# Low halves of the weights: subtracted on GpSimd in place of VectorE

## The reference

```python
for layer in range(2):
    mod = silu(c) @ ada_w[layer] + ada_b[layer]            # 2048 x 6144
    shift, scale, gate = split(mod, 3)
    h = rms_norm(x, norm_w[layer]) * (1 + scale) + shift
    if layer == 0:   # 8 heads of differential attention, 8 heads of a gated delta rule
        proj = h @ ev_w_in                                 # 2048 x 8208
        y = concat([attention * silu(z_a), delta_rule * silu(z_b)]) @ ev_w_out
    else:            # 32 query heads, 4 key/value heads, window of 128
        proj = h @ od_w_in                                 # 2048 x 4608
        y = (window_attention * silu(z)) @ od_w_out
    x = x + gate * y
return rms_norm(x, final_norm_w)
```

## Time and profile before

| | |
|---|---|
| time, median of 3 runs (range) | 2211.67 us (2211.31 to 2215.06) |
| profiled execution, its time | 2208.63 us |
| its span, first to last instruction | 2206.6 us |
| mean granted TensorE clock | 0.978 |
| TensorE matmul / weight load busy | 94% / 71% |
| VectorE, ScalarE, GpSimd busy | 51%, 34%, 0% |
| DMA, mean | 123 GB/s |

### The profile page before, as it was taken

The page is one execution under the profiler, slowest core; times in us unless marked ns, Lnnn a source line. Parts: engine busy times, 40 slices in busy tenths (PEclk is TensorE's granted clock), DMA queues, the critical chain, the costliest instruction groups (busy, mean ns, idle before and its releaser), DMA issues.

```text
span 2206.6 us, 31295 instructions
## 1 busy us (share of the span) xinstructions
PE 2081.4 (94%) x11503; PEld 1569.1 (71%) x11503; DVE 1125.2 (51%) x2030; ACT 752.7 (34%) x1547; POOL 0.2 (0%) x4
## 2 busy tenths in 40 slices
PE   6889999999999999999999799989999999998997
PEld 3257777677776767777677577767777777776875
DVE  1256575665747656475565422254445444453332
ACT  2443242422424224242243322263343333342222
POOL 0000000000000000000000000000000000000000
PEclk9999999999999999999999999999999999999998
DMA  8874333243342433433342143331212212212322
GB/s 307 334 307 157 119 125 137 104 144 116 115 144 97 142 116 116 143 115 125 116 141 80 53 148 131 121 124 58 77 64 75 81 57 81 72 42 101 119 95 105
DMA packets 59774, 270.48 MB, mean 123 GB/s; under 512 B 7411, under 2 KB 7797, under 8 KB 41589
## 3 DMA queue, kind: packets, MB, share of 16 engines
q1 hardware_dynamic: 59636, 268.64, 34.5%
HBM read 255.51 MB, written 13.11 MB: 122 GB/s over the span
## 4 chain that ended last, share of the span: by engine, by line
PE 82%; DVE 6%; issue 4%; ACT 4%; DMA 3%; SPq 1%; DVEq 0%; ACTq 0%
PE psum L562 22%; PE psum L564 20%; PE psum L563 20%; PE psum L692 3%; PE psum L931 3%; DMA ada_p<-in_ada_first 1%; PE psum L603 1%; PE psum L959 1%; PE psum L943 1%; ACT w_hi L1045 1%; PE psum L796 1%; PE psum L742 1%; PE psum L751 1%; PE psum L591 1%; DVE ada_acc L1419 1%
## 5 line engine op out<-in xcount | busy, mean ns | idle before, releaser
L562 PE MATMUL psum<-mov_hi,w_hi 128*128 128x512 f32 x2128 | 895.8, 421 | 36.1 <-DVE mov_lo L1432 11.3
L564 PE MATMUL psum<-mov_hi,w_lo 128*128 128x512 f32 x2128 | 841.3, 395 | 0.0
L563 PE MATMUL psum<-mov_lo,w_hi 128*128 128x512 f32 x2128 | 839.0, 394 | 0.0
L562 PEld LDWEIGHTS psum<-mov_hi,w_hi 128*128 128x128 f32 x2128 | 404.2, 190 | 174.5 <-issue 71.2
L564 PEld LDWEIGHTS psum<-mov_hi,w_lo 128*128 128x128 f32 x2128 | 404.0, 190 | 90.8
L563 PEld LDWEIGHTS psum<-mov_lo,w_hi 128*128 128x128 f32 x2128 | 406.1, 191 | 80.9 <-issue 8.6
L1382 DVE TENSOR_TENSOR w_lo<-w_raw,w_hi 128x512 fp32r<-128x512 f32 x532 | 354.0, 686 | 179.8 <-ACT w_hi L1045 177.1
L1045 ACT ACTIVATE w_hi<-w_raw 128x512 fp32r<-128x512 f32 x532 | 310.2, 619 | 5.5 <-DMA w_raw<-in_w_pack 5.5
L1419 DVE SCALAR_TENSOR_TENSOR ada_acc<-ada_t,silu_c,ada_acc 128x512 f32<-128x512 f32 x240 | 177.9, 741 | 3.0 <-DVE cq L1513 1.5
L1744 DVE SCALAR_TENSOR_TENSOR res<-psum,mod,xr 128x512 f32 (+1 forms) x32 | 24.0, 751 | 204.1 <-PE psum L564 202.6
L1314 ACT ACTIVATE pr<-pr,st 128x256 f32<-128x256 f32 x128 | 63.6, 498 | 136.8 <-DVE st L1791 136.8
(11 more groups left out here) (272 smaller groups left out, 1794.7 us busy)
## 6 DMA issues: line engine op xcount, KB each, us to landing
w_raw<-in_w_pack SPq DMA_DIRECT2D x133, 1024.0 KB, 5.2
ada_t<-in_ada_late SPq DMA_DIRECT2D x128, 512.0 KB, 3.3
x_in<-in_ada_first SPq DMA_DIRECT2D x32, 512.0 KB, 6.7
ada_t<-in_ada_first SPq DMA_DIRECT2D x16, 512.0 KB, 7.5
ada_p<-in_ada_first SPq DMA_DIRECT2D x16, 512.0 KB, 8.6
xr<-x_spill SPq DMA_DIRECT2D x32, 256.0 KB, 2.7
x_in<-in_x SPq DMA_DIRECT2D x4, 1024.0 KB, 6.7
x_spill<-res SPq DMA_DIRECT2D x1, 4096.0 KB, 18.3
```

The lines of the kernel that those rows point to most:

```text
L562: mm(PJ[r], w_hi[r][:, ks], mov_hi[:, kt], start=(j == 0), stop=False)
L563: mm(PJ[r], w_hi[r][:, ks], mov_lo[:, kt], start=False, stop=False)
L564: ins = mm(PJ[r], w_lo[r][:, ks], mov_hi[:, kt], start=False, stop=(j == KC - 1))
```

## The change

`split_lo` and all its calls leave VectorE's program. GpSimd gets a program that goes through the 133 blocks and their four quarters in order, in straight code without a loop. The waits are on the same semaphore at the same values, and the same semaphore is raised, so TensorE, ScalarE and SP are unchanged. The operation, its tiles and its sizes are the same.

```diff
+        @block.gpsimd
+        def _(pool):
+            for n in range(N_END):
+                r = w_ring(n)
+                for q in range(4):
+                    pool.wait_ge(w_hi_ok, 4 * n + q + 1)
+                    c = slice(q * 4 * P, q * 4 * P + 4 * P)
+                    nc.gpsimd.tensor_tensor(w_lo[r][:, c], w_raw[r][:, c], w_hi[r][:, c].bitcast(F32), ALU.subtract)\
+                        .then_inc(w_lo_ok, 1)
...
-            def split_lo(n0, m, it, q):
-
-                r = w_ring(n0)
-                dve.wait_ge(w_hi_ok, it * (4 * m) + (4 * n0 + q + 1))
-                c = slice(q * 4 * P, q * 4 * P + 4 * P)
-                V.tensor_tensor(w_lo[r][:, c], w_raw[r][:, c], w_hi[r][:, c].bitcast(F32), ALU.subtract)\
-                    .then_inc(w_lo_ok, 1)
...
-            for n in (N_BA, N_L0):
-                for q in range(4):
-                    split_lo(n, 0, 0, q)
...
                     if s % 2 == 0:
                         ada_slot(h, s)
-                    else:
-                        split_lo(N_L0 + s // SLOTS + 1, 8, h, s % SLOTS // 2)
...
-                if s < SLOTS and s % 2 == 1:
-                    split_lo(N_OUT0 + 1, 0, 0, s // 2)
...
-                    for q in range(4):
-                        if not (last_n and c == 1) and not (split and c == 0):
-                            split_lo(n0 + c + 1, 2, i, q)
...
-                    if s % 2 == 1:
-                        split_lo(N_L1 + s // SLOTS + 1, 8, g, s % SLOTS // 2)
```

More of the change, by code:

```diff
@@ L1753, in _ @@
             out_chunks(7, N_OUT0, 0, xr, 0, 32)
-            for q in range(4):
-                split_lo(N_KV + 1, 0, 0, q)
             V.scalar_tensor_tensor(out=modA[:, KC:2 * KC], in0=mod[:, 64:80], scalar=1.0,
@@ L1763, in _ @@
             norm_split(h1 + osq, rstd1, 2 * KC, range(KC))
-            for c in range(1, 4):
-                for q in range(4):
-                    split_lo(N_KV + c + 1, 0, 0, q)
             dve.wait_ge(vup_ok, 1)
@@ L1842, in _ @@
                                     mov_hi[:, k * T:k * T + T].bitcast(F32), ALU.subtract).then_inc(lo_ok, 1)
-                if s < 4:
-                    split_lo(N_OUT1 + 1, 0, 0, s)
             def token_major(i, c):
```

## The result

The changed kernel takes 2222.57 us (median of 20 runs, 2213.46 to 2224.93) against 2211.8 (20 runs of the kernel before beside it): ratio 1.0043, 95% interval 1.0031 to 1.0055. I had forecast 2202.5. The profiled execution took 2222.83 us, its span is 2220.8 (before 2208.63 and 2206.6).

A forecast was written before the change was run, and what follows sets the result against it. TensorE was taken as the bound, busy 2081.4 of 2206.6 us. Stalls -5.8, clock -8.5, latency +1.2, tail -0.6 and meetings +4.5 sum to -9.2 us: 2202.5 us against the median, range 2189 to 2236.

The forecast's parts named there:

- rivals 2: Each subtraction leaving VectorE's queue is paid back as an equal block, ada_acc stays late: +2.9, 2214.5 us; chance 0.22.
- rival 3: GpSimd holds VectorE up ahead of L815 and L787, two blocks in each of seven heads: +18.8, 2230.5 us; chance 0.29.
- Subtractions, and their price on GpSimd: GpSimd's 532 subtractions were taken at 1.3 us each, its rate hidden behind 11.0 us of matmuls per weight block.
- Seven stalls for `ada_acc`, -5.8: TensorE's seven waits of about 1 us at L815: six were to go, saving 5.8 us.
- margin of 1.65: Time ada_acc would be ready before TensorE comes for it at L815, once four subtractions left VectorE: 1.65 us.
- Clock, -8.5: Six half-clock windows after L815 go (-10.2 us), one new one elsewhere (+1.7): net -8.5 us.
- the six windows: Half-clock stretches of 3.5 us after L815 in six heads, priced at 1.7 us each, all expected to go.
- Latency, +1.2 at two places: Where TensorE waits for w_lo's first quarter, including an output projection's start, the slower subtraction costs 2 x 0.6 us.
- Tail of layer 0, -0.6: One VectorE subtraction of 0.60 us, a link of the chain at 1215.58 us, goes: -0.6 us.
- Meetings at the attention's turn, +4.5: At L787, pa meets one GpSimd subtraction, costing 0.65 us in each of seven heads: +4.5 us.
- "Not moved": the 7.2 us for `vnew`: TensorE's waits for vnew at the head loop's turn, 7.2 us, stay because no subtraction stands in front.
- Layer 1, 0: In layer 1 VectorE's normalising product starts just before GpSimd's subtraction, so GpSimd waits and nothing changes: 0 us.

The follow-up runs named there:

- 132: Kernel before with 132 already-met waits put ahead of VectorE's head loop (body 314–643): 2204.61 us, ratio 0.9945.
- 148: Kernel before with 148 already-met waits put ahead of VectorE's head loop (body 322–651): 2193.66 us, ratio 0.9912.
- 230 waits: Kernel before with 230 already-met waits put ahead of VectorE's head loop (body 363–692): 2191.40 us, ratio 0.9901.
- eight pieces: Changed kernel, but from the third weight block GpSimd subtracts only eight 8-column pieces per quarter, the rest left out: 2190.61 us, ratio 0.9916.
- halves: Changed kernel with each quarter's GpSimd subtraction split into two instructions of 256 columns: 2198.95 us, ratio 0.9946.

## Why the prediction was wrong

The sign was wrong, though 2222.6 lies in the range, between rivals 2 and 3. By its own steps:

- **Subtractions, and their price on GpSimd.** Right: 1.29 us against 1.3; the engine's rate does not bind.
- **Seven stalls for `ada_acc`, -5.8.** This is the step that failed: +4.4. I had priced two to four meetings at the mean of 0.65 us, 1.3 to 2.6 against a margin of 1.65. The trace has four blocks in this stretch, each of 0.8 to 1.1 us, 4.0 in all. The mean of half a subtraction was wrong because the two engines take turns: an instruction either comes at the start of a subtraction or behind one that had to wait itself, and pays most of it both times. That is rival 3 by mechanism and place.
- **Clock, -8.5.** Mis-sized: the share lost at the half level grew from 2206.6 x 0.022 = 49 to 56 us, +7. The stalls stayed, and of the six windows behind them four stayed too (328, 598, 867 and 1004 us); others came or grew elsewhere. A longer stall did not bring a window each time: behind L815 at 462 and 732 us TensorE had waited just as long and the clock stayed up. With the wait at 0.6 us or gone (132, 148 and 230 waits, eight pieces, halves) none of the six stands.
- **Latency, +1.2 at two places.** Mis-sized: at the two places the waits went from 3.4 to 4.2 and from 2.8 to 4.8 us, +2.8, and the third place, k and v, +4.8, was denied ("hidden, and so are the weight loads on SP's queue"). I had looked at the rate of the loads, not at what stands behind one in SyncE's order.
- **Tail of layer 0, -0.6.** Came out +2.6. The half clock behind the head loop lasts 10.2 us there (from 1208.7) against 3.4 before (from 1206.9), which at half speed is 3.4 us; what made it longer no run took apart.
- **Meetings at the attention's turn, +4.5.** The row for L787 is unchanged at 3.5 us. Too dear there, while head 0, which I had not priced at all, cost 4.8: GpSimd made five subtractions from 149.0 us on, as VectorE made four `ada_acc` and the gates. It ends in TensorE's new wait at L654.
- **"Not moved": the 7.2 us for `vnew`.** Wrong. I had seen that VectorE's own branch was late and not asked why. It is about -20 us with what hangs on it, the small stalls of the body among them, and hid two thirds of the loss.
- **Layer 1, 0.** Right: L1786 has its 1225 ns, no wait for it appeared.

My forecast had a gain where there was a loss; that the total came within 1%, and inside the range, is luck owed to the fetches. With a long turn the changed kernel would by my estimate (2211.8 + 31) have been near 2243, above the range.

## What to carry to other kernels

Moving work to GpSimd doesn't free VectorE where both read SBUF: what was paid here is 0.8 to 1.1 us of a GpSimd instruction of 1.29 at most meetings, in front of two-input operations and of copies from SBUF. So count the meetings on the critical path and price each near a whole GpSimd instruction, not at half of one, and if the work must go there, cut it into short instructions. An "issue" gap behind a loop's branch is a row like any other: compare the body's length and start with the instruction pages, since any edit that adds or removes instructions can move it over a boundary and be credited or blamed for it. And for each wait that gets longer, read the order of the queue it stands in.

## What the runs showed of the hardware

- A loop body of 330 VectorE instructions costs 0.3 us a turn where it starts at 322 or 363 of the trace's count and 3.3 to 4.4 us where it starts at 248, 280, 314 or 504, with five packets of 8 KB fetched in each turn of the kernel before. The small stalls of 0.35 us stand some 128 instructions apart (317, 447, 575) and only in bodies with a long turn. Read as pairs of such blocks, the pairs begin at 320, 576 and 832. The Trainium skill (Runtime: NRT & Kernel Launch, "Instruction fetch mechanics") calls the crossing of a page mostly hidden; here it was 0.35 us each in these bodies.
- Two waits for a semaphore that is already raised become one VectorE instruction and take 0.1 us.
- GpSimd's subtraction of 128x512 takes 1.29 us, of 128x256 0.74, of 128x8 0.20 (0.16 from start to start in a row).
- The product of L1591, with one operand in PSUM, is not held up by GpSimd (687 ns beside 688). Copies from SBUF are: 1515 ns beside 420 at L1537.
